# The low weights' pass of a split-float32 matmul moved from its shared PSUM bank to a bank of its own, in three of five stages

## The reference

```python
h = rms_norm(x, norm_mix_g)
proj = h @ w_in                      # 2048 x 10240
# three branches of width 512 (HGRN2, S5, stick-breaking attention) and three gates
merged = sum(gate_k * (branch_k @ w_branch[k]) for k in range(3))
x = x + merged @ w_out               # 2048 x 2048
hf2 = rms_norm(x, norm_ffn_g)
up = causal_depthwise_conv(hf2 @ w_up, conv_w)        # 2048 x 11264, then width 3
x = x + (silu(up[..., :D_FF]) * up[..., D_FF:]) @ w_down   # D_FF = 5632
```

## Time and profile before

| | us |
|---|---|
| runs, median (lowest, highest) | 1472.32 (1472.12, 1472.53) |
| the profiled execution, its own time | 1471.41 |
| its span, first to last instruction | 1469.7 |
| PE busy | 1414.2 (96%) |
| DVE busy | 1079.3 (73%) |
| ACT busy | 761.9 (52%) |
| POOL busy | 380.2 (26%) |

### The profile page before, as it was taken

How to read it: one execution, slowest core, us unless ns; L and a number is a source line. 1 busy time by engine, 2 the same in 40 slices (tenths; PEclk the granted TensorE clock), 3 DMA queues, 4 the chain that set the end, 5 groups by cost and what they waited for, 6 DMA issues and landing times.

```text
span 1469.7 us, 24906 instructions
## 1 busy us (share of the span) xinstructions
PE 1414.2 (96%) x8320; PEld 1248.5 (85%) x8320; DVE 1079.3 (73%) x1370; ACT 761.9 (52%) x1050; POOL 380.2 (26%) x337
## 2 busy tenths in 40 slices
PE   5999999998888989999999999999999999999999
PEld 4889888887666878998888888888888888888887
DVE  5897757879999957777668777777777776544543
ACT  5564456675344445444565555555555554444432
POOL 5044312254966631332211111111111110000000
PEclk9999999999998999999999999999999999999999
DMA  7555544453434455565556555656555555666663
GB/s 216 175 175 170 166 151 161 150 182 108 144 128 151 151 165 195 200 214 186 187 173 205 194 183 188 197 181 194 191 181 197 187 186 187 182 213 202 189 202 111
DMA packets 74338, 261.45 MB, mean 178 GB/s; under 512 B 8560, under 2 KB 9104, under 8 KB 74160
## 3 DMA queue, kind: packets, MB, share of 16 engines
q1 hardware_dynamic: 73152, 256.41, 54.0%
q0 software_dynamic: 992, 4.37, 0.8%
q10 hardware_dynamic: 144, 0.01, 0.0%
HBM read 258.66 MB, written 2.10 MB: 177 GB/s over the span
## 4 chain that ended last, share of the span: by engine, by line
PE 76%; DVE 14%; issue 4%; POOL 2%; ACT 2%; DMA 1%; SPq 0%; POOLq 0%; ACTq 0%; DVEq 0%
PE bank L295 48%; PE bank L297 25%; DVE w_lo L841 5%; DVE tmp L849 3%; PE pair L328 2%; DVE tmp L1092 2%; DVE tmp L856 1%; DMA gates<-xT 1%; PE bank L309 1%; ACT w_hi L570 1%; POOL proj L1280 1%; POOL merged L1371 1%; POOL merged L1373 1%; DVE gates L846 0%; DVE proj L846 0%
## 5 line engine op out<-in xcount | busy, mean ns | idle before, releaser
L841 DVE TENSOR_TENSOR w_lo<-raw,w_hi 128x1024 fp32r<-128x1024 f32 x500 | 632.1, 1274 | 321.0 <-ACT w_hi L570 317.2
L570 ACT ACTIVATE w_hi<-raw 128x1024 fp32r<-128x1024 f32 x500 | 512.1, 1030 | 438.7 <-PE bank L297 380.1
L295 PE MATMUL bank<-a_in,w_hi 128*128 128x512 f32 x1536 | 553.9, 401 | 42.7 <-DVE w_lo L841 40.8
L295 PE MATMUL bank<-h,w_hi 128*128 128x512 f32 x1408 | 488.4, 390 | 0.0
L297 PE MATMUL bank<-a_in,w_lo 128*128 128x256 f32 x1536 | 438.8, 286 | 0.0
L297 PE MATMUL bank<-h,w_lo 128*128 128x256 f32 x1408 | 397.1, 282 | 0.0
L295 PEld LDWEIGHTS bank<-a_in,w_hi 128*128 128x128 f32 x1536 | 295.2, 192 | 114.6 <-issue 35.5
L295 PEld LDWEIGHTS bank<-h,w_hi 128*128 128x128 f32 x1408 | 264.2, 188 | 55.4
L297 PEld LDWEIGHTS bank<-a_in,w_lo 128*128 128x128 f32 x1536 | 297.2, 194 | 0.5 <-issue 0.5
L297 PEld LDWEIGHTS bank<-h,w_lo 128*128 128x128 f32 x1408 | 266.1, 189 | 0.0
L295 PE MATMUL bank<-act,w_hi 128*128 128x512 f32 x704 | 244.1, 390 | 0.0
(11 more groups left out here) (165 smaller groups left out, 1083.3 us busy)
## 6 DMA issues: line engine op xcount, KB each, us to landing
raw<-w_up SPq DMA_DIRECT2D x176, 512.0 KB, 3.3
raw<-w_in SPq DMA_DIRECT2D x160, 512.0 KB, 4.0
raw<-w_down SPq DMA_DIRECT2D x80, 512.0 KB, 4.3
raw<-w_out SPq DMA_DIRECT2D x32, 512.0 KB, 3.8
raw<-w_br SPq DMA_DIRECT2D x16, 512.0 KB, 3.6
raw<-w_br SPq DMA_DIRECT2D x16, 256.0 KB, 3.4
raw<-w_down SPq DMA_DIRECT2D x16, 256.0 KB, 2.7
gates<-xT SPq DMA_DIRECT2D x4, 512.0 KB, 10.4
```

What stands on the lines that cost most here:

```text
L295: pe.matmul(bank[b][:, :], w[:, k * P:(k + 1) * P], a.rearrange("p a t -> p (a t)"), start=first and n == 0, stop=False, skip_group_check= ...
L570: act_e.activation(w_hi[s][:, 0:blocks * P], raw[s][:, 0:blocks * P], ACT.Copy).then_inc(hi_ready, 1)
L841: ve.tensor_tensor(w_lo[s][:, w], raw[s][:, w], w_hi[s][:, w].bitcast(F32), ALU.subtract).then_inc(lo_ready, 1)
```

## The change

In the out, up and down stages the lo pass writes to `low[j]`, 256 columns in one of the four banks that make up `pair`, with a start flag of its own on its first matmul. The bank's left half now holds hi*hi alone. `add_thirds` takes the place of `add_halves` there: DVE adds the bank's left half and `half`, waits for that, and adds `low[j]`, which then increments `tile_summed`. The product of norm2 moves to the second half of the bank that `low[3]` lies in; PE waits, ahead of the fourth tile of up, until DVE has read it. The in and GLU stages keep the shared bank, and the branch stage is as it was.

```diff
--- before.py
+++ after.py
@@ -196,6 +196,8 @@
 
         def product(name):
             return pair[M[name] % 2]
+
+        low = [pair[b // 2][:, b % 2 * 512:b % 2 * 512 + SEQ] for b in range(BANKS)]
 
 
         sems = {}
@@ -285,17 +287,18 @@
 
         @block.tensor
         def _(pe):
-            def piece(b, p, c, blocks, rhs, first, last):
+            def piece(b, p, c, blocks, rhs, first, last, low=None):
 
                 if p is not None:
                     pe.wait_ge(lo_ready, p + 1)
                 w, l = w_hi[c % RING], w_lo[c % RING]
                 for n, k in enumerate(blocks):
                     a = rhs(n)
+                    end = last and n == len(blocks) - 1
                     pe.matmul(bank[b][:, :], w[:, k * P:(k + 1) * P], a.rearrange("p a t -> p (a t)"),
-                              start=first and n == 0, stop=False, skip_group_check=True)
-                    mm = pe.matmul(bank[b][:, 0:SEQ], l[:, k * P:(k + 1) * P], a[:, 0, :],
-                                   start=False, stop=last and n == len(blocks) - 1, skip_group_check=True)
+                              start=first and n == 0, stop=end and low is not None, skip_group_check=True)
+                    mm = pe.matmul(bank[b][:, 0:SEQ] if low is None else low, l[:, k * P:(k + 1) * P], a[:, 0, :],
+                                   start=first and n == 0 and low is not None, stop=end, skip_group_check=True)
                 return mm
 
             def branch_piece(b, p, c, lo, src):
@@ -495,19 +498,22 @@
                     bank_free(i * BANKS + (OUT_T + j))
                     for h in range(2):
                         mm = piece(j, i * (2 * BANKS) + (OUT_P + 2 * j + h), 2 * j + h, range(PIECE),
-                                   lambda k: after("merged_lo", j, PIECE * h + k, a_in), h == 0, h == 1)
+                                   lambda k: after("merged_lo", j, PIECE * h + k, a_in), h == 0, h == 1, low[j])
                         mm.then_inc(piece_used, 1)
 
             def up_body(i):
                 for j in range(BANKS):
                     bank_free(i * BANKS + (UP_T + j))
+                    if isinstance(i, int) and j == 3:
+                        wait_taken(pe, "norm2")
                     for h in range(2):
                         mm = piece(j, i * (2 * BANKS) + (UP_P + 2 * j + h), 2 * j + h, range(PIECE),
-                                   lambda k: after("h2_lo", j if isinstance(i, int) else 1, PIECE * h + k, h2), h == 0, h == 1)
+                                   lambda k: after("h2_lo", j if isinstance(i, int) else 1, PIECE * h + k, h2), h == 0, h == 1, low[j])
                         mm.then_inc(piece_used, 1)
                     if isinstance(i, int) and j == 0:
                         pe.wait_ge(S("x1_sq_sum"), KT)
-                        fp32_product("norm2", [((0, P, 0, SEQ), ones[:, :], root[:, :], True, True)])
+                        pe.matmul(pair[1][:, 768:1024], ones[:, :], root[:, :], start=True, stop=True, skip_group_check=True)\
+                            .then_inc(product_done, 1)
 
             up_body(0)
             with pe.Fori(1, UP_TILES // BANKS) as i:
@@ -523,7 +529,7 @@
                         if j == 0:
                             pe.wait_ge(S("act_lo"), at + blocks)
                         mm = piece(j, i * (BANKS * len(DOWN_PIECES)) + (DOWN_P + c), c, range(blocks),
-                                   lambda k: act[:, at + k, :, :], at == 0, at + blocks == FT)
+                                   lambda k: act[:, at + k, :, :], at == 0, at + blocks == FT, low[j])
                         mm.then_inc(piece_used, 1)
                         at += blocks
                         c += 1
@@ -842,8 +848,15 @@
 
             def add_halves(n, j, dest):
 
-                ve.wait_ge(half_copied, n + 1 - (BR_TILES if isinstance(n, int) is False or n >= OUT_T else 0))
+                ve.wait_ge(half_copied, n + 1)
                 ve.tensor_tensor(dest, bank[j % BANKS][:, 0:SEQ], half[j % 2][:, :], ALU.add).then_inc(tile_summed, 1)
+
+            def add_thirds(n, j, dest):
+
+                ve.wait_ge(half_copied, n + 1 - BR_TILES)
+                ve.tensor_tensor(dest, bank[j][:, 0:SEQ], half[j % 2][:, :], ALU.add).then_inc(S("two_summed"), 1)
+                ve.wait_ge(S("two_summed"), n + 1 - OUT_T)
+                ve.tensor_tensor(dest, low[j], dest, ALU.add).then_inc(tile_summed, 1)
 
             def tt(name, out_, a, b, op):
                 link(ve, ve.tensor_tensor(out_, a, b, op), name)
@@ -873,7 +886,8 @@
 
                 wait_product(ve, name)
                 n_feat = D_MODEL if name.startswith("norm") else P
-                taken(ve.tensor_scalar(out_, product(name)[:, 0:of], 1.0 / n_feat, EPS, ALU.mult, ALU.add), name)
+                src = pair[1][:, 768:1024] if name == "norm2" else product(name)[:, 0:of]
+                taken(ve.tensor_scalar(out_, src, 1.0 / n_feat, EPS, ALU.mult, ALU.add), name)
                 wait_taken(ve, name)
 
             def exact_exp(out_, x):
@@ -1192,7 +1206,7 @@
                         else:
                             lo(i, 2 * BANKS, OUT_P + 2 * (j + 2) + c)
                     t = i * BANKS + j
-                    add_halves(i * BANKS + (OUT_T + j), j, convd[:, j, :])
+                    add_thirds(i * BANKS + (OUT_T + j), j, convd[:, j, :])
                     ve.wait_ge(tile_summed, i * BANKS + (OUT_T + j + 1))
                     ve.wait_ge(S("x1_landed"), 16)
                     ve.tensor_tensor(x1[:, t, :], x1[:, t, :], convd[:, j, :], ALU.add).then_inc(S("x1_ready"), 1)
@@ -1239,7 +1253,7 @@
                         token_norm("norm2")
                     if not (first and j < 2):
                         ve.wait_ge(S("up_scaled"), i * BANKS + (j - 1))
-                    add_halves(i * BANKS + (UP_T + j), j, sum_u[:, j % 2, :])
+                    add_thirds(i * BANKS + (UP_T + j), j, sum_u[:, j % 2, :])
                     if pair_due:
                         hidden(q, j)
                     if not (first and j == 0):
@@ -1263,7 +1277,7 @@
                         if not last or p < BANKS * n_p:
                             lo(i, BANKS * n_p, DOWN_P + p, DOWN_PIECES[p % n_p])
                     t = i * BANKS + j
-                    add_halves(i * BANKS + (DOWN_T + j), j, convd[:, j, :])
+                    add_thirds(i * BANKS + (DOWN_T + j), j, convd[:, j, :])
                     ve.wait_ge(tile_summed, i * BANKS + (DOWN_T + j + 1))
                     ve.tensor_tensor(x1[:, t, :], x1[:, t, :], convd[:, j, :], ALU.add).then_inc(S("y_ready"), 1)
```

## The result

The changed kernel takes 1477.45 us (median of 6 runs, 1477.08 to 1477.80), the kernel before on the same chip 1472.42. The ratio is 1.0035 with a 95% interval of 1.0024 to 1.0045: slower by 5.0 us, clear of no change, and inside the predicted range of 1472.7 to 1481.0, 2.1 us above the predicted 1475.3.

What follows compares the result with a forecast made beforehand. PE was taken to bound out, up and down, its matmuls running back to back. Tail 0.45 plus wait 2.4 makes 2.85 us, 1472.3 + 2.85 = 1475.2, predicted as 1475.3 for the clock; range 1472.7 to 1481.0.

Steps and rivals of the forecast that it cites:

- PE's part: Out, up and down: the lo pass writing another bank with its own start flag costs and saves PE nothing.
- p = 0.455: Time in us that the second, dependent add puts on DVE's chain per tile in out, up and down.
- The DVE-bound rival with 0.57: Up stage: second add costs 0.57 us, PE waits 12.3 us in all, 1485; chance 0.17 of more than 5 us.
- the reserve: Up stage: DVE's closed chain takes 10.185 us per two tiles against PE's 11.09; two adds make it 11.095.
- the early delay: Start of up: the norm holds DVE up, so low weights are ready late; with the change never caught up.
- the leads of 8 and 10: Early up pieces: w_lo ends 0.94 and 1.1 us before PE needs it; piece 10 loses p and 0.1.
- break-even: Up stage: p of 0.427 us, below which DVE recovers the lead and only the tail remains.
- The wait at the fifth piece of down, 2.4 us: Its w_lo, after 86 adds in up, is ready at 1235.3; PE needs it at 1232.95, so waits 2.4 us.
- The tail, 0.45: After the last matmul: half copy, add, x1 add and store depend on each other; one more add costs 0.45 us.
- The clock: Spell of about half clock after PE's wait in down, costing about 1.6 us; given 2 in 10 of the forecast.
- Out: Out's loop: DVE's reserve of 0.37 us per tile, p 0.09 more, lead shrinks by 1.1 us; nothing charged.
- The norm2 product: After up's first tile: it can start late by p at most; taken at nothing.

Runs made afterwards that it cites:

- e1: Changed kernel with DVE's add of the low product left out, so only PE's writing to its own bank remains: 1472.02 us, ratio 0.9999.
- e6: Kernel before with two more dependent DVE adds per tile, in the up stage alone: 1515.46 us, ratio 1.0292.
- e5: Kernel before with a second, dependent DVE add of 64 columns instead of 256 in out, up and down: 1472.66 us, ratio 1.0005.
- e7: Changed kernel with ACT's two functions of the norm2 factor made plain copies, saving their table loads: 1473.66 us, ratio 1.0012.
- e3: Changed kernel with the change kept in the up stage alone, out and down having their old code: 1476.12 us, ratio 1.0021.
- e8: Changed kernel with w_hi and w_lo of down's fifth and sixth pieces computed before the drain of the last up tiles: 1473.30 us, ratio 1.0009.
- e2: Kernel before with DVE's add done twice in out, up and down, the second waiting for the first: 1475.97 us, ratio 1.0026.

## Why the prediction was right, and where it was off

**PE's part, nothing.** Right, and shown by e1.

**p = 0.455.** The second add follows the first by 0.453 us, the next operation follows it by 0.341, where it was 0.334 behind the single add: 0.46 in all. The wait computed in the loop cost nothing more. The DVE-bound rival with 0.57 needed a price that was not there; e6 shows its mechanism at a price that is.

**Up: the reserve is gone and the early delay stays.** Right: the leads of 8 and 10 are 0.89 and 0.58 (forecast: hardly changed, and about 0.5), and they never recover. e5 (price below the break-even) and e7 (smaller delay) show both halves of it. In the changed kernel's own trace the turn is 11.102 us, a hundredth longer than PE's, and the lead wears down by 0.3 us over the stage; in e3, e7 and e8, with the same code in up, it is 11.093. I have no cause for this hundredth. It is the size of the margin itself, and sets the wait to 2.0 or 2.4 us. Nor is it explained why in those three the turn equals PE's so closely: over the last 29 turns the lead moves by no more than 0.015 us, at 0.68 (e3, e8) as well as at 1.94 (e7). A chain that does not depend on PE would do that only by chance, so the prediction's picture of it holds to a hundredth of a us per turn and not beyond.

**The wait at the fifth piece of down, 2.4 us.** 2.6 by starts, which is how the prediction worked it out; 2.42 by the list of waits. DVE's w_lo ended at 1236.97; the forecast's 1235.3, moved by the 1.4 us of the earlier stages that were no part of it, is 1236.7. That it came so close is in part luck. 86 adds make 0.4 us of each 0.005 us of p, and e3, with the same adds in up, waits 0.4 us less.

**The tail, 0.45.** 0.46.

**The clock: the term that was mis-sized.** I gave the spell 2 chances in 10 and so left it out of the likeliest time. All three profiles with a wait of 2.0 to 2.4 us there have it, at 1.7 us each. With it the sum is 1472.4 + 4.6 = 1477.0 against 1477.45. The price was right and the chance was wrong: the reason I gave, that the wait would stand alone, did not protect it. The trace of before had more to say than the earlier trace rows. In its in stage PE also waited 2.8 us, up to 415.9, and then had a granted clock of 0.53 for 3.4 us; behind waits of 1.6 us (up to 438.4) and 1.8 us (up to 506.3) it was 1.00. Both of its waits between 2 and 3 us had the spell, which spoke for more than 2 in 10.

**Out.** The lead there was to shrink by 1.1 us over the loop. It falls from 4.62 to 4.16 once, at the loop's start, and stays. I had read the reserve off the idle time of 0.37, but the distance between the two w_lo operations was 1.58 where it needs 1.14: the reserve was 0.44, about p. The distance between starts is the measure, since an operation's idle time and its duration overlap. It changed nothing in the sum.

**The norm2 product** was taken at nothing; it is the 0.12 us above.

## What to carry to other kernels

The idle share of an engine is not its reserve. DVE idled for 22% of a turn and could have gone only 8% faster; idling for 16% it had nothing left. So follow the closed chain of an iteration through all engines, take its length while it catches up after a disturbance (10.19 us here, against the bound engine's 11.09), and compare what is to be added with that difference. Below it an addition is free but for the kernel's end (e5), above it every turn pays in full (e6), and just at it the kernel loses the ability to recover, so that the damage shows at the next tight hand-over, here 470 us later. A stall in the bound engine can also cost its clock; when the cause sits in a fixed order of work, moving the one late item ahead (e8) gets most of it back.

## What the runs showed of the hardware that was not expected

- Two passes that accumulate into one PSUM bank, one of them over half its columns, run exactly as fast as into two banks: 0.2283 and 0.1183 us between starts in both. What the Trainium skill's page Perfetto Trace Analysis says in Matmul Optimizations of using all 8 banks bought nothing here.
- Waits of PE of 2.0, 2.1 and 2.4 us in an otherwise full stretch (e3, e2 and the changed kernel) were each followed by 3.3 to 3.4 us at 1.2 GHz. One of 3.1 us, in e6 at the same place, was not: the windows of PE over it and behind it show a granted clock of 1.00. In e6 PE had waited many times before; whether that matters is not shown.

```profile
1273.00:1277.00 4.00, 0.94 (x6) 1.00 0.03 13
1277.00:1280.00 3.00, 2.94 (x17) 1.00 0.60 178
```
